# Rotary embedding of q in a two-layer decoder: the half-swap on ScalarE's copies in place of a TensorE product

## What is computed

```
q, k, v = jnp.split(x @ w_in, 3, axis=-1)
q = apply_rope(q.reshape(B, T, DIFF_HEADS, 2, DIFF_HD), cos, sin)
k = apply_rope(k.reshape(B, T, DIFF_HEADS, 2, DIFF_HD), cos, sin)
...
x1, x2 = jnp.split(xf, 2, -1)
return jnp.concatenate([x1 * cos - x2 * sin, x2 * cos + x1 * sin], -1)
```

## Time and profile before

| | us |
|---|---|
| median of three runs | 1420.54 |
| the profiled execution | 1420.63 |
| its span on the chip | 1418.9 |
| attention, first rotation to last | 837 to 992 |
| TensorE busy | 1383.6 (98% of the span) |
| VectorE busy | 869.4 (61%) |
| ScalarE busy | 635.3 (45%) |
| GpSimd busy | 80.8 (6%) |

### The profile page before, as it was taken

One profiled execution on the slowest core, in us unless ns is written; L12 is line 12 of the kernel. 1 busy time (PEld: TensorE's weight loads), 2 busy tenths in 40 slices (PEclk: granted clock), 3 DMA queues, 4 the chain that ended last, 5 costly groups with the idle time before them and its releaser, 6 DMA issues.

```text
span 1418.9 us, 20021 instructions
## 1 busy us (share of the span) xinstructions
PE 1383.6 (98%) x7038; PEld 1135.0 (80%) x7038; DVE 869.4 (61%) x1362; ACT 635.3 (45%) x1033; POOL 80.8 (6%) x91
## 2 busy tenths in 40 slices
PE   8799999999999999999999999999999999999997
PEld 7688888888788888888888776667788888888886
DVE  4576677777586666666425537777686666664226
ACT  5666556666224444443212235666424444443211
POOL 3000000000000000000002011111000000000002
PEclk9999999999999999999999999999999999999999
DMA  6222111211222333334332222121223333334231
GB/s 195 55 65 68 45 51 52 63 55 60 75 60 67 100 100 89 103 96 152 105 104 74 89 60 60 45 74 59 90 60 89 89 103 92 100 118 134 89 104 60
DMA packets 157728, 118.85 MB, mean 84 GB/s; under 512 B 5899, under 2 KB 145645, under 8 KB 157677
## 3 DMA queue, kind: packets, MB, share of 16 engines
q1 hardware_dynamic: 157676, 118.17, 27.7%
HBM read 116.04 MB, written 2.11 MB: 83 GB/s over the span
## 4 chain that ended last, share of the span: by engine, by line
PE 90%; DVE 5%; ACT 3%; DMA 1%; issue 1%; SPq 0%; DVEq 0%; ACTq 0%
PE bank L1666 13%; PE bank L1668 13%; PE bank L1667 13%; PE bank L1681 10%; PE bank L1654 8%; PE bank L1655 8%; PE bank L1656 8%; PE bank L1735 3%; PE bank L2062 1%; PE bank L1742 1%; PE bank L2080 1%; PE bank L1733 1%; PE bank L2023 1%; PE bank L1751 1%; PE bank L1632 1%
## 5 line engine op out<-in xcount | busy, mean ns | idle before, releaser
L368 DVE TENSOR_TENSOR w_lo<-raw,w_hi 128x1024 fp32r<-128x1024 f32 x194 | 237.7, 1227 | 241.9 <-ACT w_hi L363 236.6
L1666 PE MATMUL bank<-x_hi,w_hi 128*128 128x512 f32 (+1 forms) x912 | 348.6, 382 | 2.6 <-DVE x_lo L1042 2.0
L1668 PE MATMUL bank<-x_hi,w_lo 128*128 128x512 f32 (+1 forms) x912 | 340.5, 373 | 0.0
L1667 PE MATMUL bank<-x_lo,w_hi 128*128 128x512 f32 (+1 forms) x912 | 340.2, 373 | 0.0
L363 ACT ACTIVATE w_hi<-raw 128x1024 fp32r<-128x1024 f32 x186 | 195.1, 1051 | 166.6 <-PE bank L1656 139.5
L1666 PEld LDWEIGHTS bank<-x_hi,w_hi 128*128 128x128 f32 x912 | 172.2, 189 | 33.8 <-DVE x_lo L1042 2.4
L1667 PEld LDWEIGHTS bank<-x_lo,w_hi 128*128 128x128 f32 x912 | 172.3, 189 | 30.2 <-issue 1.9
L1668 PEld LDWEIGHTS bank<-x_hi,w_lo 128*128 128x128 f32 x912 | 172.0, 189 | 30.4
L1654 PE MATMUL bank<-w_hi,u_hi 128*128 128x512 f32 x416 | 164.2, 395 | 0.6 <-DVE w_lo L368 0.6
L1656 PE MATMUL bank<-w_hi,u_lo 128*128 128x512 f32 x416 | 162.0, 389 | 0.0
L1655 PE MATMUL bank<-w_lo,u_hi 128*128 128x512 f32 x416 | 161.9, 389 | 0.0
(11 more groups left out here) (294 smaller groups left out, 2000.2 us busy)
## 6 DMA issues: line engine op xcount, KB each, us to landing
raw<-in_ffn_w_up SPq DMA_DIRECT2D x88, 512.0 KB, 3.8
raw<-in_ffn_w_down SPq DMA_DIRECT2D x44, 512.0 KB, 3.3
raw<-in_gdn_w_in SPq DMA_DIRECT2D x32, 512.0 KB, 4.1
raw<-in_diff_w_in SPq DMA_DIRECT2D x24, 512.0 KB, 3.8
raw<-in_gdn_w_out SPq DMA_DIRECT2D x8, 512.0 KB, 3.3
raw<-in_diff_w_out SPq DMA_DIRECT2D x8, 512.0 KB, 3.3
x_tok<-in_x SPq DMA_DIRECT2D x4, 512.0 KB, 5.9
ROW<-decay_rows SPq DMA_DIRECT2D x8, 256.0 KB, 4.6
```

What stands on the lines that cost most here:

```text
L368: nc.vector.tensor_tensor(w_lo[:, s, :], raw[:, (base + r) % RAW, :], w_hi[:, s, :].bitcast(F32), ALU.subtract).then_inc(lo_ready, 1)
L1666: nc.tensor.matmul(out, hi, x_hi[:, k, cols], start=(k == 0), stop=False)
L1667: nc.tensor.matmul(out, hi, x_lo[:, k, cols], start=False, stop=False)
L1668: ins = nc.tensor.matmul(out, lo, x_hi[:, k, cols], start=False, stop=last)
```

## The change

TensorE no longer rotates q. `take` of q raises a new semaphore `q_taken` in place of `bank_read[0]`, and GpSimd's cosine pass waits for that. ScalarE's new `swapped(g)` makes the swapped q itself: four copies of 32 partitions from `bank[0]` to other partitions of `rope2[0]`, with the sign in the scale; the last raises `bank_read[0]`. It stands behind `turned_p(3)` and ahead of the `take` of k, so it reads `bank[0]` much later than `take` does. VectorE's sine pass of q reads `rope2[0]` in place of a bank and waits for `bank_read[0]`; `rope(h + 1, 0)` is moved behind the clip. k is left as it was, but for its count in `rot_pe`.

```
+            def swapped(g):
+                if not (isinstance(g, int) and g == 0):
+                    act.wait_ge(rope_head, R_DVE0 + RD_N * (g - 1) + RD["qr"])
+                for b in range(4):
+                    src, dst = slice(32 * (b ^ 1), 32 * (b ^ 1) + 32), slice(32 * b, 32 * b + 32)
+                    ins = nc.scalar.activation(rope2[0][dst, :], bank[0][src, :], ACT.Copy,
+                                               scale=HD ** -0.5 * (1.0 if b % 2 else -1.0))
+                ins.then_inc(bank_read[0], 1)
...
                 turned_p(3)
+                if more:
+                    swapped(h + 1)
...
             take(0, 0)
+            swapped(0)
             split_hi(act, C_QK, 0, 2)
...
-                dve.wait_ge(rot_pe, 2 * g + kind + 1)
-                nc.vector.tensor_tensor(rope2[kind][:, :], bank[4 + kind][:, :], sin[:, :], ALU.mult).then_inc(rope_head, 1)
+                if kind == 0:
+                    wait_read(dve, 0, T_QK // 2 + g)
+                    nc.vector.tensor_tensor(rope2[0][:, :], rope2[0][:, :], sin[:, :], ALU.mult).then_inc(rope_head, 1)
+                else:
+                    dve.wait_ge(rot_pe, g + 1)
+                    nc.vector.tensor_tensor(rope2[1][:, :], bank[5][:, :], sin[:, :], ALU.mult).then_inc(rope_head, 1)
                 dve.wait_ge(rope_head, last + RD["rope2 " + name])
                 dve.wait_ge(rope_pool, 2 * g + kind + 1)
...
                     split_lo(dve, C_QK, it, 2 * r + 5)
-                    rope(h + 1, 0)
                 else:
                     hold_lo(dve, C_ATT_OUT + 5)
                 dve.wait_ge(t_pe, 1 + h * TP_N + TP["pv"])
                 nc.vector.tensor_scalar(att_o[:, :], bank[3][:, :], ROOT_MAX, -ROOT_MAX, ALU.min,
                                         ALU.max).then_inc(n_dve, 1)
+                if more:
+                    rope(h + 1, 0)
...
                 values(2)
-                if not last:
-                    rotate(h + 1, 0)
                 turn(3)
...
-            rotate(0, 0)
             step(0, 0)
```

More of the change, by code:

```diff
@@ L315, in build @@
         t_pe, t_dve, t_act, v_head = sem("t_pe"), sem("t_dve"), sem("t_act"), sem("v_head")
+        q_taken = sem("q_taken")
         rot_pe, rope_pool, rope_head = sem("rot_pe"), sem("rope_pool"), sem("rope_head")
@@ L599, in rope_cos @@
             def rope_cos(g, kind):
-                wait_read(pool, kind, T_QK // 2 + g)
+                if kind == 0:
+                    pool.wait_ge(q_taken, g + 1)
+                else:
+                    wait_read(pool, kind, T_QK // 2 + g)
                 pool.wait_ge(rope_head, R_DVE0 - RD_N + RD_N * g + (RD["qr"] if kind == 0 else RD["kr"]))
@@ L951, in take @@
                     act.wait_ge(rope_pool, 2 * g + kind - 1)
-                nc.scalar.activation(qk_raw[kind][:, :], bank[kind][:, :], ACT.Copy,
-                                     scale=(HD ** -0.5 if kind == 0 else 1.0)).then_inc(bank_read[kind], 1)
+                ins = nc.scalar.activation(qk_raw[kind][:, :], bank[kind][:, :], ACT.Copy,
+                                           scale=(HD ** -0.5 if kind == 0 else 1.0))
+                ins.then_inc(*((q_taken, 1) if kind == 0 else (bank_read[1], 1)))
+            def swapped(g):
[6 more added lines that the diff above has]
+                ins.then_inc(bank_read[0], 1)
             def step(it, r):
@@ L2018, in project_qk, with rotate_k @@
                     block_products(kind, (C_QK + 2 * odd + kind) % WS, k, k == KT - 1)
-            def rotate(g, kind):
-                wait_read(pe, kind, T_QK // 2 + g)
-                nc.tensor.matmul(bank[4 + kind][:, :], swap[:, :], qk_raw[kind][:, :], start=True,
+            def rotate_k(g):
+                wait_read(pe, 1, T_QK // 2 + g)
+                nc.tensor.matmul(bank[5][:, :], swap[:, :], qk_raw[1][:, :], start=True,
                                  stop=True).then_inc(rot_pe, 1)
@@ L2086, in step @@
                 fill(0, 1)
-                rotate(h, 1)
+                rotate_k(h)
                 fill(1, 3)
```

## The result

The changed kernel takes 1424.14 us, the median of 18 executions (1422.24 to 1428.87), beside 1421.12 for the kernel before (18 executions, 1420.18 to 1423.79). The ratio is 1.0024, with an interval of 1.0016 to 1.0032: **slower by 0.24%**, where the prediction said 1425.5.

The account below looks back on a forecast made before the run. TensorE, busy 98% of the span, was taken as the bound, with VectorE's chain nearly level at head boundaries. Boundaries +3.3, before head 0 -1.0, clock +2.8: +5.1 on 1420.63, so 1425.7, stated as 1425.5 us; range 1417.0 to 1429.0.

Parts of the forecast that it names:

- The mechanism and its places: At head boundaries, GpSimd's cosine pass of k shuts out VectorE's add of q at six; VectorE is first at one.
- The margin: At six boundaries, q's add on VectorE starts 0.06 us behind GpSimd's cosine pass of k.
- the second rival's case: VectorE's add of q starts ahead of GpSimd's pass at all boundaries, no clock falls: 1417.2 us, chance 0.24.
- anything up to 0.6 a copy changes no term: ScalarE's four copies of q behind turned_p(3): up to 0.6 us each, the forecast's terms stay the same.
- the copies' pitch of 0.50: ScalarE's four copies follow each other at 0.50 us, starting at 901.75 and ending at 903.85.
- The cover of 0.4 us: Idle ScalarE time left between the end of the copies and k's take at a boundary: 0.4 us.
- a wait of more than 0.3: Sign against the forecast: TensorE's q product waiting more than 0.3 us for the bank that the copies read.
- The register instruction: A wait on an instruction ahead of VectorE's add of q costs 0.115 us, at six boundaries.
- The rule on SBUF and PSUM: Fixed terms of 58 cycles from SBUF, 120 from PSUM would shorten q's sine pass by 0.06 us; not adopted.
- Each boundary: Scores 0.65 us later at five head boundaries, 0.54 later at the last, 0.45 sooner at the first: +3.3 us.
- Before head 0: VectorE's q passes no longer wait for a rotation, w_lo ends sooner, kr and scores follow: -1.0 us, bounds 0 and 1.7.
- The clock: TensorE's clock falls behind one in three of six new 1.65 us gaps, 1.4 us each: +2.8 us, bounds none and +8.4.

Follow-up runs that it names:

- the exchanged waits: Changed kernel with the two waits of VectorE's rope in the other order: 1419.19 us, ratio 0.9994 to the kernel before.
- GpSimd held back: Changed kernel with GpSimd's cosine pass of k waiting for q's add and its vh copy for kr: 1419.46 us, ratio 0.9986 to the kernel before.
- the wide copy: Changed kernel with one copy of 128 partitions for ScalarE's four of 32, halves not exchanged, sign not turned: 1415.51 us, ratio 0.9962.
- the move alone: Kernel before with only VectorE's rope of q moved behind the clip; TensorE still rotates q, no ScalarE copies: 1422.85 us, ratio 1.0013.
- the second filler run: Changed kernel with six more, overwritten TensorE products ahead of the scores, only at heads 2, 4, 6 and 7: 1423.20 us, ratio 1.0015.
- the fillers: Six more, overwritten products ahead of the scores in the changed kernel: at every head 1424.71 us; only at heads 2, 4, 6, 7 1423.20 us.

## Why the prediction was right, and where it wasn't

- **The mechanism and its places held.** Of the signs that the prediction named, these came: GpSimd first at six boundaries and VectorE first at the first, the add at 1.74 and 0.69, scores waiting 1.4 us (1.6 was said). The two theories were told apart by the exchanged waits and by GpSimd held back. The Trainium skill says the same of such a pair in SBUF — State Buffer (section Who interferes with whom): a VectorE operation with two SBUF inputs contends with a GpSimd one that reads SBUF, and the order of issue decides who waits. The traces agree: 1.74 against 0.69 for VectorE, 1.82 against 1.27 for GpSimd.
- **The margin came out right by luck: two errors cancel.** The prediction had the add at clip + 1.51 and GpSimd at clip + 1.45. Measured: clip + 1.60 and + 1.53. The step from clip to sine pass was put at 0.66; free of copies it is 0.61 (the wide copy) and 0.60 (the move alone). With it the add stands at clip + 1.42, ahead of GpSimd's 1.45. That is the second rival's case, and the wide copy shows it. What turned it back was a step that the prediction had called harmless, "anything up to 0.6 a copy changes no term".
- **The failed step is the copies' pitch of 0.50.** Each takes 0.59 and the next starts only when it has ended, so four take 2.39; the first doesn't overlap the operation before it either. The bank and `rope2` are ready at 905.77, so the sine pass waits until clip + 0.78, and k's `take` is 0.08 late. The cover of 0.4 us was used up, and TensorE's q product waits for the bank at six boundaries, 0.57 each. The prediction had named a wait of more than 0.3 there as a sign against it. It costs nothing here, since the scores behind it wait for `kr` anyway.
- **The register instruction**: 0.115 was estimated from the taps. The add started 0.13 behind the sine pass with it, 0.03 to 0.04 without: 0.09 to 0.10. Exchanging the waits was worth about 4 us, since it decided the race.
- **The rule on SBUF and PSUM** (the Trainium skill, VectorE: DVE Perf Modes, section The TRN2 errata) was weighed and turned down. Rightly: q's sine pass takes 0.68 from a bank (the move alone) and 0.68 from SBUF (the wide copy), not 0.06 less.
- **Each boundary** was put at +0.65, +0.54 and -0.45; it measured +0.56, +0.48 and -0.34. Sum 2.9 for 3.3.
- **Before head 0** the prediction took 1.0 us off and the trace gives 0.54: from TensorE's last product of k to the scores it was 5.88 and is 5.34. The second `w_lo` does start when ScalarE's half is ready, as was said. But the first one is late, since ScalarE's half of it stands behind the copies, and VectorE's q passes come behind it. ScalarE, VectorE and GpSimd there:

```profile
835.45 2.39 ACT L966 ACTIVATE rope<-bank 32x512 f32<-32x512 f32 x4
837.87 1.06 ACT L364 ACTIVATE w_hi<-raw 128x1024 fp32r<-128x1024 f32 x1
```

```profile
840.82 0.69 DVE L1541 TENSOR_TENSOR qr<-rope,rope 128x512 f32<-128x512 f32 x1
841.78 1.95 DVE L369 TENSOR_TENSOR w_lo<-raw,w_hi 128x1024 fp32r<-128x1024 f32 x1 [0.27 <-ACT w_hi L364]
```

```profile
840.88 1.77 POOL L607 TENSOR_TENSOR rope<-qk_raw,cos 128x512 f32<-128x512 f32 x1 [3.94 <-ACT qk_raw L956]
```

  The first `w_lo` starts at 838.96, the q passes at 840.10. So q's add comes 0.06 ahead of GpSimd's pass of k and holds it up by 0.5, and the second `w_lo`, shut out until that pass is over, ends 0.5 later than was reckoned. With the one wide copy the q passes are done before GpSimd starts, and the stretch is 4.84, the 1.0 less of the prediction. "The copies fall into idle time" was true for ScalarE and not for who waits for it.
- **The clock** was put at two falls in six gaps, +2.8 us. Two profiles of the change show one each, 2 in 12. The stretch behind the gap of 1.40 at 954.01 in the first:

```profile
956.00:959.00 3.00, 3.00 (x12) 2.13 (x12) 2.06 (x6) 0.79 (x2) 0.00 (x0) 0.50 0.00 0
```

  From head 5's scores to head 6's it is 23.13 us there, 21.78 one head earlier: 1.4 lost, as estimated for one fall. So +1.4 a run and not +2.8, and the gaps are 1.40 and not 1.65. The one in three was taken from two gaps, and the profiles of all the runs show that this was too few to go by. The gap of 1.88 of the earlier trace rows is in all thirteen profiles, and a fall follows it in three, the change's first among them. The gap before head 0, where it is 1.64 to 2.24, had one behind it in nine of ten. Of the gaps of 1.3 to 1.4 before the later heads of the change, and the two that the second filler run leaves open, 2 of 14 had one.

The terms now add up to 2.9 - 0.54 + 1.4 = +3.8, and 3.0 were measured between the medians, 3.4 between the means (1424.75 and 1421.35). The terms without the clock, 2.4, are near the distance between the fastest execution of each kernel, 2.1. A part of the difference can be seen: the fall behind head 0 costs 1.64 in the profile before (18.87 from scores to clip, 17.23 two heads later) and 0.89 in that of the change (17.26 against 16.37), and the terms take it as equal. How the rest divides between the clock inside the attention and the falls elsewhere isn't settled.

## What to carry to other kernels

When two engines that exclude each other come ready within 0.1 us, the order of two waits can be worth several us: put the wait that comes true last directly on the instruction (see in the built program or the trace that it is there, since the order in the source had opposite effects at different heads here), and if the margin is still thin, force the order with a wait on the other engine. An operation moved off the engine that sets the pace pays only if its substitute is ready before the point where someone waits; here the same copies cost 3 us behind `turned_p(3)` and gained 6 ahead of it. And "hidden in idle time" must be read for every reader of that engine's next result, not for the engine alone.

## What was not expected of the hardware

- ScalarE's copies of 32 partitions that cross partitions don't overlap: 4 in 2.39 us, pitch 0.60, each 0.586 to 0.592 over 32 of them. The copy of 128 partitions starts 0.49 after the operation before it, which lasts 0.60. Whether the crossing or the count of partitions does it wasn't tried.
- Two waits ahead of one VectorE operation are not alike. One of them is on an instruction of its own ahead of it, and if that is the late one the add starts 0.10 (a head that is written out) to 0.14 (in the loop) after its sine pass ends; with the late one on the add it is 0.03 to 0.04.
- A race won or lost by 0.02 to 0.08 us came out alike in both profiles of the change, boundary for boundary, and in the two with the fillers.
